# Second feed-forward's down projection by seven block products for eight, in four chunks, token by token, all sums on VectorE

## The reference

```python
h = rms_norm(x, norm_mlp[l])
x = x + jnp.square(jax.nn.relu(h @ w_up[l])) @ w_down[l]     # w_up 1024x4096, w_down 4096x1024
return rms_norm(x, norm_final)
```

## Time and profile before

| | |
|---|---|
| median of 3 runs | 1496.59 us |
| the profiled execution: span, first to last instruction | 1494.7 us |
| its time beside its span | no time of its own is given for it; the median lies 1.9 us above its span |
| TensorE matmul, busy | 1485.1 us, 99%, 7240 matmuls |
| TensorE weight loads | 1226.2 us, 82% |
| VectorE | 876.2 us, 59% |
| ScalarE | 565.4 us, 38% |
| GpSimd | 24.2 us, 2% |
| DMA | 149.17 MB, 100 GB/s on average |

### The profile page before, as it was taken

The page is one execution under the profiler, slowest core; times in us unless marked ns, Lnnn a source line. Parts: engine busy times, 40 slices in busy tenths (PEclk is TensorE's granted clock), DMA queues, the critical chain, the costliest instruction groups (busy, mean ns, idle before and its releaser), DMA issues.

```text
span 1494.7 us, 20331 instructions
## 1 busy us (share of the span) xinstructions
PE 1485.1 (99%) x7240; PEld 1226.2 (82%) x7240; DVE 876.2 (59%) x1425; ACT 565.4 (38%) x836; POOL 24.2 (2%) x21
## 2 busy tenths in 40 slices
PE   9999999999999999999999999999999999999998
PEld 7878888888888888888888887888888888888887
DVE  6737764775665655443468877965665653255433
ACT  5215553333433333323325656444443331123231
POOL 0000000000000000000000000000000000000000
PEclk9999999999999999999999999999999999999999
DMA  6623222223322232333333223322122322333221
GB/s 234 226 87 97 77 91 85 85 83 101 112 88 95 98 98 98 99 102 110 113 99 106 94 97 102 110 76 84 61 81 85 109 91 96 98 99 98 99 71 57
DMA packets 44445, 149.17 MB, mean 100 GB/s; under 512 B 4792, under 2 KB 7352, under 8 KB 44260
## 3 DMA queue, kind: packets, MB, share of 16 engines
q1 hardware_dynamic: 39840, 138.43, 28.3%
q10 hardware_dynamic: 4548, 9.96, 1.9%
HBM read 146.24 MB, written 6.06 MB: 102 GB/s over the span
## 4 chain that ended last, share of the span: by engine, by line
PE 98%; issue 0%; DMA 0%; DVE 0%; ACT 0%; SPq 0%; POOLq 0%; POOL 0%; DVEq 0%; ACTq 0%
PE ps L1168 31%; PE ps L1170 31%; PE ps L1169 31%; PE ps L1319 1%; PE ps L1332 1%; PE ps L2340 1%; PE ps L1209 0%; DMA x<-x_dram 0%; PE ps L1202 0%; PE ps L2360 0%; PE ps L1377 0%; PE ps L2372 0%; PE ps L2440 0%; PE ps L2285 0%; PE ps L1274 0%
## 5 line engine op out<-in xcount | busy, mean ns | idle before, releaser
L528 ACT ACTIVATE wh<-stage 128x1024 fp32r<-128x1024 f32 x254 | 268.9, 1059 | 544.3 <-PE ps L1170 540.0
L1168 PE MATMUL ps<-hh,wh 128*128 128x512 f32 x1088 | 430.7, 396 | 0.3 <-DVE wl L764 0.3
L1170 PE MATMUL ps<-hh,wl 128*128 128x512 f32 x1088 | 424.3, 390 | 0.0
L1169 PE MATMUL ps<-hl,wh 128*128 128x512 f32 x1088 | 423.6, 389 | 0.0
L764 DVE TENSOR_TENSOR wl<-stage,wh 128x1024 fp32r<-128x1024 f32 x253 | 309.3, 1223 | 185.2 <-ACT wh L528 184.7
L1168 PEld LDWEIGHTS ps<-hh,wh 128*128 128x128 f32 x1088 | 204.3, 188 | 46.7 <-issue 3.9
L1170 PEld LDWEIGHTS ps<-hh,wl 128*128 128x128 f32 x1088 | 204.2, 188 | 43.5
L1169 PEld LDWEIGHTS ps<-hl,wh 128*128 128x128 f32 x1088 | 204.5, 188 | 39.8
L1168 PE MATMUL ps<-ah,wh 128*128 128x512 f32 (+1 forms) x448 | 171.7, 383 | 0.0
L1170 PE MATMUL ps<-ah,wl 128*128 128x512 f32 (+1 forms) x448 | 171.5, 383 | 0.0
L1169 PE MATMUL ps<-al,wh 128*128 128x512 f32 (+1 forms) x448 | 171.5, 383 | 0.0
(11 more groups left out here) (340 smaller groups left out, 1839.3 us busy)
## 6 DMA issues: line engine op xcount, KB each, us to landing
stage<-stream_dram SPq DMA_DIRECT2D x254, 512.0 KB, 3.3
bias_lines<-bias_line ACTq DMA_DIRECT2D x1, 3840.0 KB
bias<-bias_lines ACTq DMA_DIRECT2D x4, 512.0 KB, 4.8
x<-x_dram SPq DMA_DIRECT2D x3, 512.0 KB, 7.3
out_dram<-x SPq DMA_DIRECT2D x12, 128.0 KB, 1.9
bias<-bias_lines ACTq DMA_DIRECT2D x4, 256.0 KB, 2.9
mem<-mem_dram ACTq DMA_DIRECT2D x1, 1024.0 KB, 4.8
stage<-stream_dram SPq DMA_DIRECT2D x2, 256.0 KB, 4.0
```

The costliest lines, as they stand in the source:

```text
L528: A(parts_of(b, p)[0], b.stage[:, p.slot, :], ACT.Copy).then_inc(s.hi_ready, 1)
L1168: MM(out, wh, xh, start=start, stop=False, skip_group_check=True)
L1169: MM(out, wh, xl, start=False, stop=False, skip_group_check=True)
L1170: return MM(out, wl, xh, start=False, stop=stop, skip_group_check=True)
```

## The change

**Blocks.** The 4096 hidden features are worked in four chunks (`CHUNKS2`) of 1024: eight up panels, then the down projection of that chunk. In a chunk, the activations are a 2x2 of blocks: token tiles 0 and 1 or tiles 2 and 3, by even or odd feature tiles; the weights are a 2x2 as well: even or odd feature tiles by left or right 512 output columns. The product of the two needs eight block products. The change forms sums and differences of blocks and does seven (P1, Q5, P6, P2, P7, Q3, R4), each in two units A and B of two feature tiles' pairs, 14 units of 12 matmuls.

**Roles.** Activations are now loaded into TensorE (128 tokens at a time) and weights stream, 512 columns wide; results are token-major, in `y` (4 token tiles x 1024). x is turned token-major by TensorE in the first chunk, eight 128x128 transposes behind each of four up panels, and ScalarE copies it into `y` (`copy_x`).

**Activations.** VectorE evacuates an up panel with relu and norm in one operation (`up_evac`), ScalarE squares it into `mix`; every second panel VectorE makes four combinations of 256 tokens (`combine`), ScalarE copies the high parts of three single blocks and of the four combinations, VectorE makes the low parts (`single_rest`, 768 elements a partition; `sum_rest`, 1024).

**Weights of the down projection** come in four quarters of 1 MB a chunk into `raw`; VectorE adds quarters in place, eight operations a chunk (`raw_sum`). High and low parts go through the same four slots as the up panels (`unit_hi`, `unit_lo`).

**Results.** Products gather in banks 0, 1, 4 and 5; ScalarE copies P1 from banks 0 and 1 into 2 and 3 (`seed`), where further products are added. VectorE takes them into `y` in six operations a chunk (`take`). From the second chunk on the up projection uses banks 6 and 7 alone.

**End.** The last two units are done token tile by token tile. The final norm is per token, hence per partition: ScalarE squares with an accumulated sum (`y_square`), VectorE weighs by the gain (`weigh`), GpSimd raises to the power, ScalarE scales tiles 2 and 3, VectorE tiles 0 and 1. Four transfers of 512 KB write the output.

Without TensorE's lines for the up projection, which keep their work, the core of the diff is:

```diff
+UNITS2 = 14
+ITEMS2 = KT + UNITS2
+P1A, Q5A, P1B, Q5B, P6A, P6B, P2A, P2B, P7A, P7B, Q3A, Q3B, R4A, R4B = range(UNITS2)
+QUARTER = (0, 0, 0, 0, 0, 0, 3, 3, 1, 1, 2, 2, 3, 3)
+COMBINATION = (0, 3, 0, 3, 5, 5, 2, 2, 4, 4, 6, 6, 1, 1)
+PRODUCT_BANK = (0, 4, 0, 4, 0, 0, 2, 2, 0, 0, 4, 4, 0, 0)
+SUMMED = {Q5A: 1, P6A: 2, Q5B: 3, P6B: 4, P7A: 5, P7B: 6, R4A: 7, R4B: 8}
...
+class Unit2:
+    def __init__(self, c, j):
+        self.c, self.j, self.half = c, j, (j // 2) % 2 if j < P6A else j % 2
+        self.index = P_FF2 + ITEMS2 * c + KT + j
+        self.slot = self.index % RING
...
-    for half in range(2):
-        tok = slice(M * half, M * half + M)
-        for k in range(0, KT, 1 + half):
-            sp.wait_ge(s.final_scaled, KT * half + k + 1)
-            sp.dma_start(out[P * k:P * k + P, tok], b.x[:, k, tok]).then_inc(s.out_done, 16)
-    sp.wait_ge(s.out_done, 32 * KT)
+    up_rows(0, range(RING, KT))
+    sp.wait_ge(s.panel_done, P_FF2)
+    for r in range(4):
+        quarter(0, r)
+    for c in range(1, CHUNKS2):
+        up_rows(c, range(RING))
+        sp.wait_ge(s.summed.sem, s.summed.at(8 * c))
+        sp.wait_ge(s.lo_ready, Unit2(c - 1, P6B).index + 1)
+        quarter(c, 0)
+        sp.wait_ge(s.lo_ready, Unit2(c - 1, P7B).index + 1)
+        quarter(c, 1)
+        sp.wait_ge(s.lo_ready, Unit2(c - 1, Q3B).index + 1)
+        quarter(c, 2)
+        sp.wait_ge(s.lo_ready, Unit2(c - 1, R4B).index + 1)
+        quarter(c, 3)
+        up_rows(c, range(RING, KT))
+    for n, t in enumerate((2, 3, 0, 1)):
+        sp.wait_ge(s.final_scaled, n + 1)
+        sp.dma_start(out[P * t:P * t + P, :], b.scaled[:, t, :]).then_inc(s.out_done, 16)
+    sp.wait_ge(s.out_done, 16 * TT)
...
+    def unit_hi(p):
+        act.wait_ge(s.raw_in[QUARTER[p.j]].sem, s.raw_in[QUARTER[p.j]].at(16 * p.c + 16))
+        if p.j in SUMMED:
+            act.wait_ge(s.summed.sem, s.summed.at(8 * p.c + SUMMED[p.j]))
+        act.wait_ge(s.panel_done, p.index - RING + 1)
+        A(b.wh[:, p.slot, :], b.raw[:, QUARTER[p.j], p.half, :], ACT.Copy).then_inc(s.hi_ready, 1)
...
+    def combination_hi(c, m):
+        n = PAIRS2 * c + m
+        act.wait_ge(s.acted2, 2 * n + 2)
+        A(b.xch[:, m, 0:3, :], b.mix[:, 1:4, :], ACT.Copy).then_inc(s.act2_hi, 1)
+        act.wait_ge(s.combined.sem, s.combined.at(n + 1))
+        A(b.xch[:, m, 3:7, :], b.mix[:, 4:8, :], ACT.Copy).then_inc(s.act2_hi, 1)
+    def copy_x(t):
+        act.wait_ge(s.x_turned.sem, s.x_turned.at(t + 1))
+        A(b.y[:, t, :].rearrange("p (h c) -> p h c", h=2), b.ps[:, 4:6, :], ACT.Copy).then_inc(s.x_copied.sem, 1)
...
+        A(b.ps[:, 2:4, :], b.ps[:, 0:2, :], ACT.Copy).then_inc(s.seeded.sem, 1)
...
+    last = 6 * (CHUNKS2 - 1)
+    act.wait_ge(s.act2_ready, 8 * CHUNKS2)
+    act.wait_ge(s.taken.sem, s.taken.at(last + 4))
+    for t in range(2):
+        if t:
+            act.wait_ge(s.y_squared.sem, s.y_squared.at(t))
+        y_square(t, slice(T, D), t)
+    act.wait_ge(s.taken.sem, s.taken.at(last + 5))
+    for t in (2, 3):
+        act.wait_ge(s.y_squared.sem, s.y_squared.at(t))
+        y_square(t, slice(0, D), t)
+    act.wait_ge(s.pow_done, 6)
+    act.wait_ge(s.weighted.sem, s.weighted.at(2))
+    for t in (2, 3):
+        A(b.scaled[:, t, :], b.scaled[:, t, :], ACT.Copy, scale=b.rs[:, t:t + 1]).then_inc(s.final_scaled, 1)
+    for t in range(2):
+        act.wait_ge(s.taken.sem, s.taken.at(last + 6 + t))
+        act.wait_ge(s.y_squared.sem, s.y_squared.at(4 + t))
+        y_square(t, slice(0, T), 4 + t)
...
-        for u in range(4):
-            j = 4 * i + u
-            evac_row(Panel(p0 + u, RING, i), 0, b.tmp[:, u % 2, :], (e0 + u) % 4)
-            lo(Panel(p0 + u + RING, RING, i))
-            dve.wait_ge(s.evac, e0 + j + 1)
-            V.scalar_tensor_tensor(b.tmp[:, u % 2, :], b.tmp[:, u % 2, :], 0.0, b.tmp[:, u % 2, :], ALU.max,
-                                   ALU.mult).then_inc(s.acted2, 1)
-            rest(j, u % 2, base)
...
-                    if m == 1:
-                        V.tensor_tensor(b.x[:, k, :], b.x[:, k, :], b.ps[:, (e0 + c) % 4, :],
-                                        ALU.add).then_inc(s.evac, 1)
-                    lo(p.plus(RING))
...
+        V.scalar_tensor_tensor(b.tmp[:, u % 2, :], b.ps[:, bank, :], 0.0, b.rrow[:], ALU.max,
+                               ALU.mult).then_inc(s.evac, 1)
+    def combine(c, m):
+        dve.wait_ge(s.acted2, 2 * (PAIRS2 * c + m) + 2)
+        st.mark(V.tensor_tensor(b.mix[:, 4, :], b.mix[:, 0, :], b.mix[:, 2, :], ALU.subtract))
+        V.tensor_tensor(b.mix[:, 5, :], b.mix[:, 1, :], b.mix[:, 0, :], ALU.subtract)
+        st.wait()
+        st.link(V.tensor_tensor(b.mix[:, 6, :], b.mix[:, 4, :], b.mix[:, 1, :], ALU.subtract))
+        V.tensor_tensor(b.mix[:, 7, :], b.mix[:, 3, :], b.mix[:, 6, :], ALU.add).then_inc(s.combined.sem, 1)
...
+        V.tensor_tensor(b.raw[:, to, half, :], b.raw[:, to, half, :], b.raw[:, other, half, :],
+                        ALU.add).then_inc(s.summed.sem, 1)
...
+        V.tensor_tensor(b.y[:, tiles, columns], b.y[:, tiles, columns], b.ps[:, bank:bank + tiles.stop - tiles.start, :],
+                        op).then_inc(s.taken.sem, 1)
...
+    for c in range(CHUNKS2):
+        for u in range(KT):
+            up_evac(c, u)
+            if u >= RING:
+                unit_lo(Unit2(c, u - RING))
+            elif c or u:
+                up_lo(Up2(c, u + RING))
+            if u % 2:
+                combine(c, u // 2)
+                single_rest(c, u // 2)
+            if u == RING:
+                raw_sum(c, 0, 1, 0, 1)
+            elif u == RING + 1:
+                raw_sum(c, 0, 2, 0, 2)
+            elif u == RING + 2:
+                raw_sum(c, 0, 1, 1, 3)
+            elif u == RING + 3:
+                raw_sum(c, 0, 2, 1, 4)
+            if u % 2:
+                sum_rest(c, u // 2)
+        unit_lo(Unit2(c, P6A))
+        unit_lo(Unit2(c, P6B))
+        unit_lo(Unit2(c, P2A))
+        raw_sum(c, 1, 2, 0, 5)
+        unit_lo(Unit2(c, P2B))
+        raw_sum(c, 1, 2, 1, 6)
+        unit_lo(Unit2(c, P7A))
+        raw_sum(c, 3, 0, 0, 7)
+        if c == 0:
+            dve.wait_ge(s.x_copied.sem, s.x_copied.at(TT))
+        take(c, 1, P6B, early, right, 0, ALU.subtract)
+        unit_lo(Unit2(c, P7B))
+        raw_sum(c, 3, 0, 1, 8)
+        take(c, 2, Q5B, late, right, 4, ALU.add)
+        unit_lo(Unit2(c, Q3A))
+        unit_lo(Unit2(c, Q3B))
+        unit_lo(Unit2(c, R4A))
+        take(c, 3, P7B, late, right, 0, ALU.subtract)
+        unit_lo(Unit2(c, R4B))
+        take(c, 4, P2B, early, left, 2, ALU.add)
+        if c < CHUNKS2 - 1:
+            up_lo(Up2(c + 1, 0))
+            take(c, 5, Q3B, early, right, 4, ALU.add)
+            up_lo(Up2(c + 1, 1))
+            up_lo(Up2(c + 1, 2))
+            take(c, 6, R4B, late, left, 0, ALU.add)
+            up_lo(Up2(c + 1, 3))
...
+    take(c, 5, Q3B, early, right, 4, ALU.add)
+    dve.wait_ge(s.taken.sem, s.taken.at(last + 5))
+    weigh(early, slice(0, D)).then_inc(s.weighted.sem, 1)
+    dve.wait_ge(s.y_squared.sem, s.y_squared.at(4))
+    V.tensor_scalar(b.mean[:, early], b.sums[:, early], 1e-6, None, ALU.add).then_inc(s.mean_ready, 1)
+    for t in range(2):
+        dve.wait_ge(s.panel_done, Unit2(c, R4A + t).index + 1)
+        V.tensor_tensor(b.y[:, t, left], b.y[:, t, left], b.ps[:, t, :], ALU.add).then_inc(s.taken.sem, 1)
+        dve.wait_ge(s.taken.sem, s.taken.at(last + 6 + t))
+        weigh(slice(t, t + 1), left).then_inc(s.weighted.sem, 1)
+        dve.wait_ge(s.y_squared.sem, s.y_squared.at(5 + t))
+        V.tensor_scalar(b.mean[:, t:t + 1], b.sums[:, t:t + 1], b.sums[:, 4 + t:5 + t], 1e-6, ALU.add,
                         ALU.add).then_inc(s.mean_ready, 1)
-    def final(half, chunks):
-        tok = slice(M * half, M * half + M)
-        dve.wait_ge(s.row_done, 6 + half)
-        for k in chunks:
-            if k < k7:
-                dve.wait_ge(s.x_second, KT + k + 1)
-                V.tensor_tensor(b.x[:, k, tok], b.x[:, k, tok], b.ps[:, 7 - half, tok],
-                                ALU.mult).then_inc(s.final_scaled, 1)
-            else:
-                dve.wait_ge(s.evac, E_END + half)
-                dve.wait_ge(s.x_squared, 48 + half)
-                V.scalar_tensor_tensor(b.x[:, k, tok], b.x[:, k, tok], col(b, "norm_final", k), b.ps[:, 7 - half, tok],
-                                       ALU.mult, ALU.mult).then_inc(s.final_scaled, 1)
-    last_sum(0)
-    last_mean(0)
-    final(0, range(0, 4))
-    last_sum(1)
-    final(0, range(4, 6))
-    last_mean(1)
-    final(0, range(6, 8))
-    final(1, range(KT))
+        dve.wait_ge(s.pow_done, 7 + t)
+        dve.wait_ge(s.weighted.sem, s.weighted.at(3 + t))
+        V.tensor_scalar(b.scaled[:, t, :], b.scaled[:, t, :], b.rs[:, t:t + 1], None,
+                        ALU.mult).then_inc(s.final_scaled, 1)
...
+    def part(p, m, t, first, last):
+        j = p.j
+        tok = slice(P * t, P * t + P)
```

(40 more changed lines are left out.)

348 lines of the change are left out of this document (181 added, 167 removed).

## The result

The changed kernel takes **1481.38 us** (median of 4 runs, 1481.15 to 1481.51), the kernel before 1496.62 beside it (4 runs, 1496.24 to 1497.07). The ratio is 0.9898, with a 95% interval from 0.9884 to 0.9912: faster by 1.0%. The forecast was 1480.2. The profiled execution has a span of 1479.4 us, against 1494.7 before.

The account below looks back on a forecast made before the run. TensorE, carrying 98% of the span, was taken to bound the kernel. Terms -22.4 - 1.1 + 4.3 + 2.8 = -16.4 gave a span of 1478.3, or 1480.2 us beside the median of 1496.59; range 1475 to 1488.

Parts of the forecast that it names:

- Part 1: Second feed-forward's down projection: 768 matmuls, the last 48 cut into 96 halves, become 672 at 0.2265 us, -22.4 us.
- the value projection of the first block does just that ... the same pace: Down projection: swapped operand roles keep the pace, as the value projection's three matmuls take 0.68 us.
- The prediction's own condition: Units of the down projection: a pace other than 0.2265 us makes the forecast wrong by 6.7 us per hundredth.
- Part 2: End of TensorE's stream: column sums and reciprocal-root spread between the last matmuls go, 0.90 + 0.22, -1.1 us.
- Part 3: First chunk: four groups of eight transposes of x cost 3.8 us, plus 0.5 for late ScalarE copies, +4.3 us.
- Rival C: Transposes of x don't overlap with what surrounds them, each 0.27 us long: 1485 us, chance 0.04.
- Part 4: Each chunk: VectorE's 65 us fit beside TensorE's 81.5 us, margins 1.5 to 2 us at three places, 0 us.
- The 16 us that the averages leave: Against small waits: VectorE's and TensorE's average work leaves 16 us of room per chunk.
- Rivals A and B: A: small waits per chunk, 1484 to 1490, chance 0.15. B: VectorE bounds TensorE, over 4.9 us lost per chunk, chance 0.05.
- Part 5: After the last matmul: later squares and scalings and a 512 KB last transfer, tail 11.2 instead of 8.4, +2.8 us.
- The sign that the prediction named: Profile after, end of TensorE's stream: the last matmul is through near 1467 us.
- Rival D: The end: transfer 1.9 to 3 us and copies never late, 1477 us; its chance lies inside the forecast's 0.75.

Follow-up runs that it names:

- experiment 1: Changed kernel with the matmuls of units P7A and P7B issued twice, 96 more in all: 1503.81 us, ratio 1.0049 to the kernel before.
- experiments 5 to 8: Changed kernel with operands moved: weights high, 1482.17 us; two weight rings, 1479.16; small tensors below weights, 1492.23; shared region realigned by 640 bytes, combinations' first parts offset, 1475.82.
- experiments 2 and 6: Changed kernel with 21 of 32 transposes of x left out, 1479.79 us; with two rings of weights, 1479.16 us, and the tail reordered too, 1476.54 us.
- experiment 3: Changed kernel with one more 512-element VectorE operation behind each unit's rest, 1486.02 us; with two, 1520.21 us.
- the fastest kernel: Changed kernel with 640 bytes of small tensors moved to the shared region's end and the tail reordered: 1471.47 us, ratio 0.9833 to the kernel before.

## Why the prediction was right

Its result was 1.2 us low (1480.2 for 1481.4). Not all of its steps were that good.

- **Part 1, down projection, -22.4.** The count of matmuls was right (experiment 1 prices each at its pitch), the pace was not. The step that failed is "the value projection of the first block does just that ... the same pace". The earlier trace rows are right, but the property they were taken to show, operands in changed roles, isn't the one that decides. The value projection has both operands low and in phase; the units have their weights low and their combinations 640 bytes beside (experiments 5 to 8). 672 x 5.7 ns = +3.8 us, so the term is -18.6. The prediction's own condition, 6.7 us for each hundredth of a microsecond in the pace, sized it correctly. The kernel before held the counter-evidence: its first down projection.
- **Part 2, norm work in the stream, -1.1.** Nothing contradicts it; it wasn't tried by itself.
- **Part 3, transposes, +4.3.** Four groups of 0.87 us and 0.08 us behind each are in the trace: 3.8. Of the 0.5 for late copies nothing came; experiments 2 and 6 show that the fourth group was within a microsecond of it. Rival C (0.27 us for each transpose, 1485) has fallen by the rows of 0.87, in which each starts 0.109 us behind the one before. The Trainium skill ("TensorE: Matmul & The Clock Gate", Part 4) gives about 275 ns for a transpose within a kernel. As the duration of one this trace agrees with it (270 to 273 ns); as a price for each in a row it does not hold here.
- **Part 4, VectorE feeds TensorE, 0.** TensorE waits for nothing. VectorE's durations add up to 64.9 us in chunk 1, and 65 were worked out; the windows show 61.4 busy of 82.6, since neighbours overlap. The single durations held: takes out of two banks 1.22 us, three-block rests 0.95, the copy between banks 1.01. The 16 us that the averages leave were never there for the units, where VectorE is busy 32.2 of 39.0 us. One more 0.75 us operation behind each unit's rest costs 4.6 us in all, two cost 38.8 (experiment 3). Rivals A and B are mechanisms that exist: A sets in with some 10 us more VectorE work per chunk, B's 19 us lie between 10 and 21 us more.
- **Part 5, the tail, +2.8.** The order of events is the predicted one, link by link. The size is +1.2: the tail is 9.6 us, not 11.2. VectorE's last operation ends 6.55 us behind the last matmul, worked out were 7.3 (12.7 - 5.4). Some 0.2 of that is a slip of adding: the steps behind Q + 10.2 (0.82, 0.16, 0.6, 0.69) give Q + 12.5. The read of the accumulator, taken as a step behind the square, starts before the square has ended (1471.52, the square's end 1471.61). From there to the end 3.0 us pass, not 3.9: the last 512 KB transfer takes 2.6 us and not the 3.3 of a load. By the formula of the Trainium skill ("DMA: Bandwidth & Descriptors", Anatomy of one DMA) it would grow by 0.9 over the 1.9 of 128 KB; the sum had 1.4, and 0.7 was measured, so the formula was the nearer.
- **The sum.** -22.4 + 3.8 - 1.1 + 3.8 + 1.2 = -14.7, beside a measured difference of spans of 15.3; the stage began 0.4 us earlier in the profiled execution of the changed kernel, by its first operand loads. Two errors, +3.8 in part 1 and -2.1 in parts 3 and 5, went against each other: that the number came within 1.2 us is in part luck. The sign that the prediction named shows it: the last matmul was to be through near 1467 and was at 1469.84.
- **The range.** Rival D's 1477 doesn't follow from its own terms: no late copy (-0.5) and a transfer of 1.9 us (-1.4) give 1478.3, so the low end of the range should have been 1476.3. The result doesn't depend on it.

## What to carry to other kernels

Give all tensors that TensorE reads the same start modulo 256 bytes: 640 bytes too many of small tensors ahead of a shared region cost this kernel 7.7 us (1479.19 with the reordered tail alone, 1471.47 with both), and no wait, idle time or busy share in the profile shows it, only the distance from one matmul's start to the next. When a pace is taken from another phase, compare where its operands lie, not only their shapes and roles. And read the load of an engine that feeds the bound in the stage in which it feeds it: VectorE looked 84% busy over a chunk when it was 97% busy in the units, and there it held TensorE up.

## What the runs showed of the hardware that was not expected

- The pace of 512-wide matmuls depends on the start addresses of the operands against each other: 226.7 ns with no difference, 226.8 with 256 bytes in two thirds of the held operands, 232.1 to 232.9 with 64 or 128 there, and with 640 bytes (128 modulo 256) 230.5 in the first down projection, 232.3 in the units and 233.3 in up panels. Why these three differ is open, and so is whether it is the load of the next operand beside the stream of this one that collides; offsets under 64 bytes were not tried.
- The offset isn't all: behind a break in TensorE's stream the first matmuls are slower with operands in phase too. In the fastest kernel, from 124.4 us on, behind a group of small matmuls, the starts are 338, 235, 229, 232 and 231 ns apart, then 226 to 227.
- Six transfers out, four of them of 256 KB, end no earlier than four of 512 KB (7.8 us behind the last matmul's start in both), and four that leave within 3.7 us take 2.6 to 4.1 us each instead of 2.6 to 2.8.
- A wait of TensorE of 4.1 us is followed by twelve matmuls at 0.427 us (granted clock 0.50), one of 2 us isn't.
